# Second step's weight sums moved into the projection before it, one product order for all steps, and half of the first job's second matrix put ahead of a gather

## The reference, cut to what matters

```python
# experts of the first block: each token goes to 4 of 32 experts
hh = xb @ w1[e] + b1[e]                      # 1024 -> 2048
y  = swiglu_clamped(hh) @ w2[e] + b2[e]      # 1024 -> 1024
# each layer of the second block
x = x + mixer(rmsnorm(x, norm_mix_g)).astype(x.dtype)    # ends in "@ w_out"
h = rmsnorm(x, norm_ffn_g)
x = x + (silu(h @ w1) * (h @ w3)) @ w2       # 1024 -> 2816 twice, 2816 -> 1024
```

## Time and profile before

| what | value |
|---|---|
| median of three runs | 2014.79 us |
| profiled execution, whole | 2010.76 us |
| its span | 2009.0 us |
| TensorE busy (matmul) | 1932.0 us, 96% |
| VectorE busy | 590.5 us, 29% |
| ScalarE busy | 353.9 us, 18% |
| moved by DMA | 563.95 MB |
| mean granted TensorE clock | 0.991 |

### The profile page before, as it was taken

How to read it: one execution, slowest core, us unless ns; L and a number is a source line. 1 busy time by engine, 2 the same in 40 slices (tenths; PEclk the granted TensorE clock), 3 DMA queues, 4 the chain that set the end, 5 groups by cost and what they waited for, 6 DMA issues and landing times.

```text
span 2009.0 us, 25933 instructions
## 1 busy us (share of the span) xinstructions
PE 1932.0 (96%) x10093; PEld 1220.4 (61%) x10094; DVE 590.5 (29%) x1070; ACT 353.9 (18%) x752; POOL 29.0 (1%) x50
## 2 busy tenths in 40 slices
PE   7999899999999999999999999999999999999998
PEld 4876444433334443443333348787888899888887
DVE  1441311110111111111111123454433377544332
ACT  1231211110111111111011023431010120310101
POOL 2200000000000000000000000000000000000000
PEclk8999899999999999999999999999999999999999
DMA  9949499999989979999999997333545433335420
GB/s 355 312 176 384 189 376 421 422 422 421 422 359 392 422 311 422 422 421 422 422 422 422 422 388 235 105 105 106 188 148 167 148 125 105 110 121 182 147 70 22
DMA packets 170670, 563.95 MB, mean 281 GB/s; under 512 B 10758, under 2 KB 110376, under 8 KB 118128
## 3 DMA queue, kind: packets, MB, share of 16 engines
q1 hardware_dynamic: 167648, 554.96, 71.4%
q0 software_dynamic: 2192, 7.34, 1.3%
q10 hardware_dynamic: 768, 0.76, 0.1%
HBM read 561.97 MB, written 1.05 MB: 280 GB/s over the span
## 4 chain that ended last, share of the span: by engine, by line
PE 79%; DMA 13%; SPq 4%; DVE 2%; issue 1%; ACT 1%; DVEq 0%
PE psum L855 15%; DMA ring<-in_w_dram 12%; PE psum L1205 11%; PE psum L883 9%; PE psum L1287 7%; PE psum L1333 6%; PE psum L998 5%; SPq L454 4%; PE psum L705 4%; PE psum L634 3%; PE psum L826 2%; PE psum L842 2%; PE psum L1232 2%; PE psum L1354 1%; PE psum L864 1%; DMA ring<-in_w_ada_dram 1%
## 5 line engine op out<-in xcount | busy, mean ns | idle before, releaser
L855 PE MATMUL psum<-ring,arena 128*64 128x512 f32 x2176 | 490.7, 596 | 37.7 <-DMA ring<-in_w_dram 37.7
L855 PEld LDWEIGHTS psum<-ring,arena 128*64 128x64 f32 x2176 | 152.0, 137 | 368.7 <-issue 253.1
L883 PE MATMUL psum<-ring,arena 128*64 128x512 f32 x1088 | 241.7, 597 | 3.2
L2124 DVE TENSOR_SCALAR arena<-psum 128x512 f32<-128x512 f32 x34 | 23.5, 692 | 731.0 <-PE psum L864 731.0
L883 PEld LDWEIGHTS psum<-ring,arena 128*64 128x64 f32 x1088 | 77.7, 137 | 145.5 <-issue 145.5
L1287 PE MATMUL psum<-arena,ring 128*128 128x256 f32 x640 | 141.7, 379 | 0.0
L1287 PEld LDWEIGHTS psum<-arena,ring 128*128 128x128 f32 x640 | 121.4, 190 | 16.4
L1205 PE MATMUL psum<-arena,mixT 128*128 128x256 f32 x528 | 122.7, 383 | 5.3 <-DVE arena L2340 4.8
L1571 ACT ACTIVATE arena<-arena 128x512 f32<-128x512 f32 x34 | 21.4, 630 | 546.4 <-DVE arena L2124 546.3
L1205 PEld LDWEIGHTS psum<-arena,mixT 128*128 128x128 f32 x528 | 99.6, 192 | 19.4 <-DVE arena L2321 6.5
L1205 PE MATMUL psum<-ring,hT 128*128 128x256 f32 x352 | 84.0, 381 | 0.9 <-ACT arena L1784 0.9
(11 more groups left out here) (415 smaller groups left out, 1981.2 us busy)
## 6 DMA issues: line engine op xcount, KB each, us to landing
ring<-in_w_dram SPq DMA_DIRECT2D x384, 1024.0 KB, 22.6
ring<-in_ffn_w_dram SPq DMA_DIRECT2D x66, 1024.0 KB, 5.3
ring<-in_w_ada_dram SPq DMA_DIRECT2D x24, 1024.0 KB, 11.3
ring<-in_odd_w_in_dram SPq DMA_DIRECT2D x16, 1024.0 KB, 5.5
ring<-in_even_w_in_dram SPq DMA_DIRECT2D x13, 1024.0 KB, 12.7
ring<-in_w_in_dram SPq DMA_DIRECT2D x12, 1024.0 KB, 17.8
ring<-in_w_out_dram SPq DMA_DIRECT2D x4, 1024.0 KB, 14.7
ring<-in_even_w_out_dram SPq DMA_DIRECT2D x4, 1024.0 KB, 5.1
```

Source lines behind the costliest of these rows:

```text
L855: mm = nc.tensor.matmul(bank[4 + q][64 * h:64 * h + 64, :], xg[:, k, SLOTS * r:SLOTS * (r + 1)], ring[(C_MOE + k) % RING][:, (2 * h + q) * ...
L883: mm = nc.tensor.matmul(bank[7][64 * h:64 * h + 64, :], act_T[:, at:at + 64], w[:, k, 512 * h:512 * h + 512], start=(f == 0), stop=(f == 7))
```

## The change

There are two independent parts.

In `first_job`, three `keep_busy` matmuls are put ahead of `turn_act(0)`. Chunks 8 and 9 of the second matrix of job 0 are put directly behind `turn_act(0)`, ahead of the gather for job 1; chunks 10 and 11 stay where the whole second matrix stood.

In the feed-forward parts, step 0 gets the product order of the other steps, with the last `column_sums` by itself between P1 and P6. The weight sums of step 1 leave step 0's VectorE list and are made in `add_projection`, after its first of four parts. Counting functions for the semaphores (`product_at`, `split_at`, `mixed_at`) follow.

```diff
 PRODUCTS = ("P1", "P6", "P5", "P7", "P2", "P4", "P3")
-FIRST_PRODUCTS = ("P1", "P2", "P6", "P5", "P7", "P4", "P3")
 def split_at(s, name):
-    return 4 * (s + (s >= 1) + (s > FFN_STEPS)) + SPLITS.index(name) + 1
+    return 4 * (s + (s >= 2) + (s > FFN_STEPS + 1)) + SPLITS.index(name) + 1
 def mixed_at(layer, n):
-    return 4 * ((FFN_STEPS + 1) * layer + 1) + n
+    return 4 * ((FFN_STEPS + 1) * layer + 2) + n
...
-            def second_matrix(weights, e):
+            def second_matrix(weights, e, chunks=range(8, 12)):
                 pe.wait_ge(S.act_saved, e + 1)
-                for j in range(8, 12):
+                for j in chunks:
...
                 mm.then_inc(S.gates_turned, 1)
+                keep_busy(3, bank[7])
                 turn_act(0)
+                second_matrix(0, 0, range(8, 10))
                 pe.wait_ge(S.picks_built, 2)
                 gather_one(1, range(KT), lambda k: bank[0][:, SLOTS * k:SLOTS * (k + 1)]).then_inc(S.gathered, 1)
...
-                second_matrix(0, 0)
+                second_matrix(0, 0, range(10, 12))
...
                     def p2():
-                        def ready(k):
-                            if k == 2:
-                                column_sums(3 + 2 * layer, 3)
-                            pe.wait_ge(S.g_ready, KT * (1 + 2 * layer) + 4 + k + 1)
                         pe.wait_ge(S.ffn_kept, s + 1)
-                        product(homes[0], x_blocks[:, 4:8, 0:P], wa[:, 4:8, :], False, None if i else ready) \
+                        product(homes[0], x_blocks[:, 4:8, 0:P], wa[:, 4:8, :], False) \
...
                     p1()
                     if i == 0:
-                        p2()
+                        column_sums(3 + 2 * layer, 3)
                     p6()
                     p5()
...
                     p7()
-                    if i:
-                        p2()
+                    p2()
                     p4()
                     p3()
...
-            def add_projection(first, j0, col):
+            def add_projection(first, layer, j0, col):
                 for j in range(4):
                     dve.wait_ge(S.chunk_done, first + j + 1)
                     ...
                     only_gained(j, col, hT)
+                    if j == 0:
+                        split_weights(first + 4, layer, 1)
...
                         V.reciprocal(ffn_r, ffn_r).then_inc(S.y_scale, 1)
                         dve.wait_ge(S.y_scale, layer + 1)
-                        split_weights(first, layer, 1)
```

More of the change, by code:

```diff
@@ L121 @@
 PRODUCTS = ("P1", "P6", "P5", "P7", "P2", "P4", "P3")
-FIRST_PRODUCTS = ("P1", "P2", "P6", "P5", "P7", "P4", "P3")
 SPLITS, SUMS = ("T1", "T2", "T3", "T4"), ("u2", "u3", "c22", "c21", "c12")
-def products_of(i):
-    return PRODUCTS if i else FIRST_PRODUCTS
 def product_at(s, name):
-    return 6 * s + products_of(s % FFN_STEPS).index(name) + 1
+    return 6 * s + PRODUCTS.index(name) + 1
 def split_at(s, name):
-    return 4 * (s + (s >= 1) + (s > FFN_STEPS)) + SPLITS.index(name) + 1
+    return 4 * (s + (s >= 2) + (s > FFN_STEPS + 1)) + SPLITS.index(name) + 1
 def mixed_at(layer, n):
-    return 4 * ((FFN_STEPS + 1) * layer + 1) + n
+    return 4 * ((FFN_STEPS + 1) * layer + 2) + n
 def sum_at(s, name):
@@ L2321, in split_weights @@
                 V.tensor_tensor(t4, b21, t2, ALU.subtract).then_inc(S.ffn_split, 1)
+            def add_projection(first, layer, j0, col):
+                for j in range(4):
+                    dve.wait_ge(S.chunk_done, first + j + 1)
+                    part = xT[:, 512 * j:512 * j + 512]
+                    V.tensor_tensor(part, part, bank[(j0 + j) % 2], ALU.add).then_inc(S.proj_saved, 1)
+                    dve.wait_ge(S.proj_saved, j0 + j + 1)
+                    only_gained(j, col, hT)
+                    if j == 0:
+                        split_weights(first + 4, layer, 1)
             def ffn(first, layer, col, dst):
@@ L2373, in _ @@
             split_weights(C_FFN0, 0, 0)
-            add_projection(C_EOUT, 30, 104)
+            add_projection(C_EOUT, 0, 30, 104)
             ffn(C_FFN0, 0, 96, gained_6)
@@ L2459, in _ @@
             split_weights(C_FFN1, 1, 0)
-            add_projection(C_OOUT, 50, 112)
+            add_projection(C_OOUT, 1, 50, 112)
             ffn(C_FFN1, 1, 120, hT)
```

## The result

The changed kernel takes 2001.95 us in the median (six runs, 1998.31 to 2007.75), against 2014.06 us for six runs of before taken with them; the ratio is 0.9934, 95% interval 0.9917 to 0.995. With seven more runs taken later the mean of 13 runs is 2002.8 us. The profiled execution took 1998.31 us, its span is 1996.5 us: 12.5 us under the span of before. Both profiled executions lie some 4 us under the mean of their kernel, so their difference is near that of the means (11.8 us).

The account below looks back on a forecast made before the run. Experts were taken as bound by the weight stream, the rest from 1200 us by TensorE. First job 5.6, even layer 4.4 and odd layer 2.9 made 12.9 us, from 2014.79 to 2001.9; range 1996 to 2009.

Parts of the forecast that it names:

- rival (a): Experts: the weight stream swallows the first job's gain; gain 7.3 us, time 2007.5, chance 0.09.
- First job, 5.6 us: End of job 0: the next gather starts at 250.85 in place of 256.47, 5.6 us sooner, filler priced at nothing.
- rival (b): First job: the clock falls all the same, as fillers may not count enough; gain 7.8 us, time 2007.0, chance 0.08.
- Job 1 and, with it, the full stream begin 5.6 us sooner: Behind the first job: nothing is moved there, so all experts were to stand 5.6 us earlier, to 1187.
- If the span from the last expert to P1 changes by more than half a microsecond: Between experts and even feed-forward: such a change was to show that the coupling had been read wrongly.
- The traffic in 243 to 248 us is full: First job: a sign that the weight stream fills the former gap; full slices stand at 422 GB/s.
- Feed-forward, 4.4 and 2.9 us: P1 to first down matrix: starts 4.4 us sooner in the even layer, 2.9 in the odd; difference put to the clock.
- The remaining waits: Feed-forward: TensorE still waits 0.9 us at P6 of step 0 and 1.1 us at P7 of step 1.
- The moved weight sums: Projection: about 4.7 us of VectorE work hides in 5.57 us of idle time, some 0.8 to spare; cost 0.
- (c): Feed-forward: the clock falls at the new short waits of both layers; gain 9.8 us, time 2005.0, chance 0.08.
- (d): Projection: weight sums wait for chunks of step 1 not yet landed, making the kernel slower; chance 0.03 with (e).
- (e): Projection: weight sums run no earlier, since VectorE reaches add_projection late; part of (d), chance 0.03 together.

Follow-up runs that it names:

- e1: Kernel before with only the first_job edit, feed-forward parts as before; 0.9969 of before, median 2010.3 us.
- e3: Changed kernel without the three filling matmuls ahead of turn_act(0); 0.9928 of before, median 2003.3 us.
- e4: Changed kernel with the filling matmuls, but all four chunks of the second matrix behind the gather as before; 0.9959 of before, median 2007.3 us.
- e7: e4 with two more filling matmuls behind turn_act(0), so both gaps are filled in the old order; 0.9947 of before, median 2003.0 us.
- e2: Changed kernel with the old first_job, so only the feed-forward part is changed; 0.9962 of before, median 2006.6 us.
- e5: Changed kernel with the weight sums of step 2 made behind c22 in step 1, not ahead of u2; 0.9935 of before, median 1999.3 us.
- e6: Changed kernel with P6, P7 and P3 of step 0 waiting for the second, third and fourth activation sum, not P6 for all; 0.9926 of before, median 1999.9 us.
- e9: The changed kernel once more, unaltered, as base in the same rounds as e10 and e11; 0.9946 of before, mean 2003.0 us.
- e10: Changed kernel with the edits of e5 and e6 together; 0.9921 of before, median 1998.1 us.
- e11: e10 with four rather than two filling matmuls in the wait at about 210 us; 0.9905 of before, median 1996.4 us.
- e8: Changed kernel with the eight shallow second-bias products mixed with the four gather blocks ahead of them; 0.994 of before, median 2002.7 us.

## Why the prediction was right, and where it was not

*The question it was built on*, whether the stream begins earlier, was answered rightly. The stream stood still for want of buffers, and what the first job gained arrived at the end of the experts, 4.7 us of it. The runs of e1 show it against the rival (a).

*First job, 5.6 us*: the gather moved by 5.67. Every step of the sum is in the trace within 0.2 us: the second matrix at 239.47 (239.45), the gather at 243.06 (242.95), L821 at 250.80 (250.85). The filler was rightly priced at nothing.

*Its reason was half right.* I took the full clock because TensorE would be idle for under 1.5 us. That was right for the whole edit, but I did not ask which half of it does the work. Leaving the filler out cost 1.7 us of work in the trace and nothing that six runs show (e3), and alone it gave no gain in the time (e4); the second gap, ahead of the gather, matters more, and can be closed with chunks or, with the first filled too, with anything else (e7). What I gave as rival (b), that the filler may not count for enough, is true of the filler alone. And what I held against (b), the full clock from 208.74 to 216.5 us in the trace of before, is weaker than it looked: five of the thirteen traces have a fall that begins at 213 to 214 us, in the same instructions.

*"Job 1 and, with it, the full stream begin 5.6 us sooner"* failed by 0.9 us. Job 1 began 5.58 sooner, but a new fall at 256 slowed its first matrix by 1.5 us and with it the release of buffers. I had set this as the test of the coupling: the shift at 262 was not the shift at 600 (the second matrix at 595.02 came at 590.31, 4.71 earlier). That the fall takes the missing part is borne out by the traces together, not by this pair. From the gather L821 to the transfer that begins at 406.62 here (its counterpart in each trace) stand 155.0 us in the mean of the four traces with no fall behind the first job (before, e2, e3, e5), 156.2 in the six with 1.7 us of lost work (changed, e1, e6, e9, e10, e11), and 158.6 in the two with 3.4 (e4, e7); but the four alone scatter over 2.6 us. The coupling stands; the clock behind the edit was taken as fixed, and it is not.

*"If the span from the last expert to P1 changes by more than half a microsecond"*: it changed by 1.1, which I had called a sign of a misread coupling. It is the even mixer's fall, in before and e2 but not in the changed run, so the sign was badly chosen: it also moves when a fall comes or goes there, whatever the coupling.

*"The traffic in 243 to 248 us is full"*: it was 320 GB/s of 422; two chunks were spread over 242.5 to 249.5 us. Why stays open. Also, was read too narrowly behind 1200 us: its slices there run from 235 down to 22 GB/s, not from 190 to 70. Nothing in the sum hangs on it.

*Feed-forward, 4.4 and 2.9 us*: 4.2 and 2.7. P6 came 3.53 us after P1 (3.51 worked out), P7 of step 1 20.65 (20.53), the down matrix 27.63 (27.41). The difference is a small one many times over: with the starts behind the waits a product took 1.74 us here, I used 1.72, and nine of them stand in the sum. The remaining waits, the weakest numbers, were 0.77 and 0.91 as the profile counts them, and 0.9 and 1.1 with start-up, as the addition had them. The 1.5 us of the even layer's fall are part of this gain only against the one trace of before; without them the two layers give 5.3 us (twice 2.67), not 6.9.

*The moved weight sums* cost nothing, with 0.90 us to spare (0.8 worked out). Rivals (c), (d) and (e) did not occur: the clock is whole in both layers of the changed kernel.

*The total* of 2001.9 against 2001.95 owes something to luck. The gain was put at 12.9 us and came out at 12.1 in the medians and 11.8 in the means; the three runs that it was taken from stood 0.7 us above the median of six. In the profiled executions the 0.9 us lost behind the first job are nearly paid by 1.1 us from a fall in the even mixer that the changed run did not have and e2, with the same feed-forward edit, did. And the gain that I set out to explain on one execution of before contains a fall in the even layer (1.5 us) that e1 did not have.

## What to carry to other kernels

A wait ahead of small matmuls costs more than its length when the clock falls behind it: here two waits of 2.9 and 2.0 us cost 5.1 us more in half-rate work. Close the later wait first, by moving work that is ready into it: that alone left 1.7 us of lost work, while closing only the earlier one left 3.4 and saved no time that the runs show. Where no work is ready, matmuls that nobody reads, in both gaps, do nearly as well. And read more than one trace before a gain is put down to the clock, since falls come and go in places that nobody edited; mind that a mark late in the trace carries every fall ahead of it, as in e1; compare marks inside the trace on both sides of the edit, and the means of many runs.

## What the runs showed of the hardware that was not expected

The clock of TensorE falls in the midst of dense work. At 256 us of the changed kernel it had been busy without a gap since 239.47, and still the granted clock went from 1.00 to 0.50 for over 3 us. Whatever the chip counts, the share of time in which TensorE is busy does not tell it alone; the last 3.4 us ahead of the fall were products only 32 rows deep, but e8 could not pin it on them. The Trainium skill (TensorE: Matmul & The Clock Gate, Part 1: The HAM clock gate) has idle time bring the half rate, and the moment of a change vary from run to run. The second is what 13 traces show; the first does not cover this fall.

Half-rate stretches come in few sizes: 1.7, 3.4 or 5.1 us of lost work in the experts of all 13 traces. And in one and the same kernel a run of 1998.31 us has a mean clock of 0.995 and one of 2007.75 has 0.990: by the slope of all runs 7.7 of these 9.4 us go with the clock. The mean clock is a rough measure all the same. The trace of e11 has 0.993 and took 1996.31 us, that of e10 0.995 and 1996.49: e11 has 8.5 us of lost work at 20 to 38 us where e10 has 5.1, and yet its filler at 208.85 starts only 0.1 us later.
